# Expert slots in tiles of 64 and 32 tokens over a ring of five experts' weights, in a hybrid retention and attention trunk

## What is computed

```python
def hier_moe(h, w_group, w_router, w_gate, w_up, w_down):
    """Top-1 expert group, then top-2 experts inside it; gated-MLP experts."""
    ...
    weights = g_w * top_p / jnp.sum(top_p, axis=-1, keepdims=True)
    expert_idx = g_sel[:, None] * EXPERTS_PER_GROUP + top_i
    gates = jnp.sum(jax.nn.one_hot(expert_idx, N_EXPERTS, dtype=jnp.float32) * weights[..., None], axis=1)
    a = jnp.einsum('td,edf->tef', t, w_gate)
    u = jnp.einsum('td,edf->tef', t, w_up)
    hid = jax.nn.silu(a) * u * gates[:, :, None].astype(t.dtype)
    y = jnp.einsum('tef,efd->td', hid, w_down)
```

## Time and profile before

| | us |
|---|---|
| median of three runs | 1501.71 |
| lowest, highest | 1496.98, 1505.82 |
| the profiled execution | 1498.73 |
| its span, first to last instruction | 1496.6 |

### The profile page before, as it was taken

The page is one execution under the profiler, slowest core; times in us unless marked ns, Lnnn a source line. Parts: engine busy times, 40 slices in busy tenths (PEclk is TensorE's granted clock), DMA queues, the critical chain, the costliest instruction groups (busy, mean ns, idle before and its releaser), DMA issues.

```text
span 1496.6 us, 14033 instructions
## 1 busy us (share of the span) xinstructions
PE 1175.5 (79%) x5748; PEld 727.3 (49%) x5748; DVE 454.4 (30%) x736; ACT 242.8 (16%) x451; POOL 302.2 (20%) x232
## 2 busy tenths in 40 slices
PE   5999999999989982777779649688868296777790
PEld 4789698897967771322223224343434232322230
DVE  4212234322581033211112162635544311111114
ACT  4122221321421110000001010213213000000011
POOL 4133132231532202000222242100000200012124
PEclk9999999999999975988889959898988588998895
DMA  6141221321302353899995163100201769999825
GB/s 241 42 155 58 83 101 56 129 68 56 141 1 94 131 225 144 328 414 424 386 397 188 67 262 133 42 0 0 77 36 63 289 237 414 427 384 403 338 74 196
DMA packets 47176, 273.32 MB, mean 183 GB/s; under 512 B 8742, under 2 KB 8870, under 8 KB 33270
## 3 DMA queue, kind: packets, MB, share of 16 engines
q1 hardware_dynamic: 21168, 151.26, 25.7%
q0 software_dynamic: 13952, 77.15, 13.0%
q10 hardware_dynamic: 12000, 44.12, 7.4%
HBM read 277.28 MB, written 35.78 MB: 209 GB/s over the span
## 4 chain that ended last, share of the span: by engine, by line
PE 58%; issue 15%; DVE 11%; DMA 7%; POOL 6%; ACT 2%; ACTq 0%; POOLq 0%; SPq 0%; DVEq 0%
PE ps L665 19%; PE ps L828 14%; PE ps L849 6%; PE ps L886 4%; PE ps L972 4%; POOL ring_r L1672 4%; DMA ring<-in_w_gu,w_row 3%; PE ps L877 3%; DMA ring<-in_w_gu 2%; PE ps L814 2%; PE ps L798 2%; PE ps L751 2%; POOL slot_rows L1696 1%; DVE xT L1218 1%; DVE arena L1599 1%
## 5 line engine op out<-in xcount | busy, mean ns | idle before, releaser
L828 PE MATMUL ps<-ring,arena 128*64 128x512 f32 x768 | 258.4, 657 | 105.5 <-issue 99.5
L828 PEld LDWEIGHTS ps<-ring,arena 128*64 128x64 f32 x768 | 81.7, 151 | 272.9 <-issue 272.9
L665 PE MATMUL ps<-x_hi,ring_r 128*128 128x264 f32 x1024 | 190.9, 287 | 7.0 <-DVE xT_r L1206 7.0
L1672 POOL TENSOR_TENSOR ring_r<-ring,ring_r 128x1024 fp32r<-128x1024 f32 x56 | 134.2, 2408 | 301.5 <-ACT ring_r L999 301.5
L1218 DVE TENSOR_TENSOR arena<-ps,gains 128x512 f32<-128x512 f32 (+1 forms) x74 | 46.7, 673 | 397.8 <-PE ps L814 384.1
L665 PE MATMUL ps<-ring_r,x_hi 128*128 128x512 f32 (+1 forms) x480 | 155.8, 406 | 11.6 <-POOL ring_r L1672 11.6
L665 PEld LDWEIGHTS ps<-x_hi,ring_r 128*128 128x128 f32 x1024 | 160.3, 189 | 7.5 <-DVE xT_r L1206 7.3
L665 PE MATMUL ps<-xT_r,ring_r 128*128 128x264 f32 x512 | 146.1, 285 | 0.0
L828 PE MATMUL ps<-arena 128*64 128x512 f32 x256 | 133.9, 683 | 0.0
L849 PE MATMUL ps<-arena 128*64 128x512 f32 x512 | 116.9, 598 | 4.3 <-ACT arena L1121 4.3
L665 PEld LDWEIGHTS ps<-ring_r,x_hi 128*128 128x128 f32 (+1 forms) x480 | 84.3, 176 | 43.3 <-POOL ring_r L1672 13.1
(11 more groups left out here) (177 smaller groups left out, 1494.9 us busy)
## 6 DMA issues: line engine op xcount, KB each, us to landing
ring<-in_w_gu SPq DMA_DIRECT2D x24, 2048.0 KB, 14.1
arena<-in_w_down SPq DMA_DIRECT2D x32, 1024.0 KB, 10.4
ring<-in_w_ret SPq DMA_DIRECT2D x48, 512.0 KB, 3.6
arena<-in_w_gu SPq DMA_DIRECT2D x8, 2048.0 KB, 19.1
arena<-slot_rows ACTq DMA_DIRECT2D x32, 512.0 KB, 7.3
slot_out<-arena ACTq DMA_DIRECT2D x32, 512.0 KB
slot_rows<-arena ACTq DMA_DIRECT2D x8, 1024.0 KB, 4.0
ring<-in_w_ret_out SPq DMA_DIRECT2D x16, 512.0 KB, 4.5
```

Source lines behind the costliest of these rows:

```text
L665: last = mm(dst, a_parts[x], b_parts[y], start=(start and n == 0), stop=(stop and n == 2))
L828: last = mm(ps[half, b, :], xgT[:, k % 2, c, half], by_row(gu(2 * k + g))[:, c, :], start=(c == 0), stop=(c == KT - 1))
L1672: G.tensor_tensor(w_lo[slot][:, m], w_raw[slot][:, m], w_hi[to][:, m], ALU.subtract).then_inc(lo_made, 1)
```

## The change

The slot buffer is laid out anew. With c tokens an expert has ceil(c/32) tiles of 32. Pairs of tiles are "doubles" of 64 slots, an odd tile is a "single" of 32. There are 16 places for doubles and 16 for singles, and place j of the singles shares the weight buffer of place j of the doubles. If a double of an expert is in place j and the expert has a single, the single goes home to place j; singles without a home take free places. `PASSES` fixes twelve rounds, each with two halves of 64 slots: two doubles, or one double and two singles, or four singles in the last. A pass with singles therefore makes products with 32 stationary columns.

The weights have a ring of five buffers, all of which are prefetched with the weights of experts 0 to 4. GpSimd then "mends" these five with ten indirect DMAs, which write only partition 0 where the place really holds that expert. SP fills places 5 to 15, with the expert's number read from `e_of` into a register, when the single that used the buffer before has been computed. After both doubles of a pair of places have been computed, GpSimd "reloads" the two buffers for the singles; partition 0 alone is written where single and double are the same expert's.

Row loads and result stores become two DMAs of 64 rows. The slot rows and their transposes move into the buffer of `xT`. DVE's slot arithmetic grows from 13 to some 45 instructions.

The diff, cut to its core:

```diff
+TILE = 32
-SLOTS_W = 4
+W_SLOTS = 5
+AHEAD = 5
+PASSES = [(("d", 0), ("d", 1)), (("d", 2), ("s", 0)), (("d", 3), ("d", 4)), (("s", 2), ("d", 5)),
+          (("d", 6), ("s", 4)), (("d", 7), ("d", 8)), (("s", 6), ("d", 9)), (("d", 10), ("s", 8)),
+          (("d", 11), ("d", 12)), (("s", 10), ("d", 13)), (("d", 14), ("d", 15)), (("s", 12), ("s", 14))]
+ROUNDS = len(PASSES)
...
+        def double_arrived(eng, arrived, l, j):
+            eng.wait_ge(arrived[j % W_SLOTS], times_filled(l, j))
+            if j < AHEAD:
+                eng.wait_ge(mended[j // 2 > 0], 16 * (l + 1) * 2 * (AHEAD - 2 if j // 2 else 2))
+        def singles_arrived(eng, arrived, l, j):
+            n = j // 2
+            eng.wait_ge(arrived[n % 2], 32 * (l * (EXPERTS // 4) + n // 2 + 1))
...
+        def column_tiles(k):
+            for n, (kind, j) in enumerate(PASSES[k]):
+                if kind == "d":
+                    yield slice(BLK * n, BLK * n + BLK), j
+                else:
+                    for g in range(2):
+                        yield slice(BLK * n + TILE * g, BLK * n + TILE * g + TILE), j + g
...
+            def experts(l):
+                m = mo[l]
+                sp.wait_ge(m["eb_ready"], 1)
+                for j in range(AHEAD, EXPERTS):
...
+                    e = sp.value_load(e_of[0:1, l, j:j + 1], min_val=0, max_val=EXPERTS - 1)
+                    gu_d, dn_d = a["w_gu"][l], a["w_down"][l]
+                    if j >= W_SLOTS:
+                        round_full(sp, l, gu_bank(pass_of("s", j - W_SLOTS)), pass_of("s", j - W_SLOTS))
+                    gate_up_weights(l, j, gu_d[bass.ds(e, 1)].rearrange("a p c -> p (a c)"))
+                    if j >= W_SLOTS:
+                        round_full(sp, l, B_YB, pass_of("s", j - W_SLOTS))
+                    down_weights(l, j, dn_d[bass.ds(e, 1)].rearrange("a p c -> p (a c)"))
...
                     for c in range(KT):
-                        for g in range(2):
-                            half = slice(BLK * g, BLK * g + BLK)
-                            last = mm(ps[half, b, :], xgT[:, k % 2, c, half], by_row(gu(2 * k + g))[:, c, :],
+                        for cols, j in column_tiles(k):
+                            last = mm(ps[cols, b, :], xgT[:, k % 2, c, cols], by_row(gu(j))[:, c, :],
                                       start=(c == 0), stop=(c == KT - 1))
...
-                        act.dma_start(xg[:, k % 2, :], slot_rows.rearrange("(b p) c -> b p c", p=2 * BLK)[k])\
-                            .then_inc(m[f"x_in{k % 2}"], 16)
+                        for n, half in enumerate(PASSES[k]):
+                            act.dma_start(xg[BLK * n:BLK * n + BLK, k % 2, :],
+                                          slot_rows[half_rows(half):half_rows(half) + BLK, :]).then_inc(m[f"x_in{k % 2}"], 16)
...
+                for j in range(AHEAD):
+                    pool.wait_ge(gu_in[j % W_SLOTS], times_filled(l, j))
+                    others(a["w_gu"], gu(j), j).then_inc(mended[j // 2 > 0], 16)
+                    pool.wait_ge(down_in[j % W_SLOTS], times_filled(l, j))
+                    others(a["w_down"], flat(down[j % W_SLOTS]), j).then_inc(mended[j // 2 > 0], 16)
+                def reload(w, dst, arrived, k):
+                    for n in range(0, EXPERTS, 2):
+                        if pass_of("d", n + 1) == k:
+                            for j in (n, n + 1):
+                                others(w, dst(j), AHEAD + j).then_inc(arrived[n // 2 % 2], 16)
+                for k in range(ROUNDS):
+                    round_full(pool, l, gu_bank(k), k)
+                    reload(a["w_gu"], gu, gu_again, k)
+                    round_full(pool, l, B_YB, k)
+                    reload(a["w_down"], lambda j: flat(down[j % W_SLOTS]), down_again, k)
```

More of the change, by code:

```diff
@@ L290, in build @@
         cv = Carve()
[L291 to L294, removed]
+        gu_arena = cv(2, KT * 512)
+        down = [*(lambda d: [d[:, n] for n in range(AHEAD)])(cv(AHEAD, 2, D))]
         yo = cv(2, D)
@@ L846, in down_project @@
                         for c in range(2):
-                            for g in range(2):
-                                half = slice(BLK * g, BLK * g + BLK)
-                                last = mm(ps[half, b, :], hidT[:, c, half],
-                                          down[:, (2 * k + g) % SLOTS_W, c, 512 * n:512 * n + 512],
+                            for cols, j in column_tiles(k):
+                                last = mm(ps[cols, b, :], hidT[:, c, cols], down[j % W_SLOTS][:, c, 512 * n:512 * n + 512],
                                           start=(c == 0), stop=(c == 1))
@@ new lines, in experts @@
+                pos = v(POSN, nt, 16)
+                V_.tensor_tensor(pos, ps[:, 2, 0:16 * nt].rearrange("p (t e) -> p t e", e=16), before[:, 0:nt, :],
+                                 ALU.add).then_inc(free[2], 1)
+                step.done(V_.tensor_reduce(v(N_, 16), passed, X, ALU.add))
+                step.done(V_.memset(v(Z16, 16), 0.0))
+                step(V_.tensor_reduce(v(D_, 16), passed[:, :, 1:THRESH:2], X, ALU.add))
+                P0, P1 = v(PP, 17)[:, 0:16], v(PP, 17)[:, 1:17]
@@ new lines, in experts @@
+                step.done(V_.tensor_tensor(v(PC, nt, 16), pos, per_expert(v(CC, 16)), ALU.add))
+                step(V_.tensor_tensor(v(DBL, nt, 16), v(DBL, nt, 16), per_expert(v(CA, 16)), ALU.mult))
+                step(V_.tensor_tensor(v(PC, nt, 16), v(PC, nt, 16), v(DBL, nt, 16), ALU.add))
+                for at in (MA, MB):
+                    step.done(V_.tensor_tensor(v(at, nt, 16), v(at, nt, 16), v(PC, nt, 16), ALU.mult))
+                step.wait()
+                place = v(SLOT, 2, 5)
@@ new lines, in experts @@
+                for n, at in enumerate((MA, MB)):
+                    step.done(V_.tensor_reduce(place[:, n, 0:nt], v(at, nt, 16), X, ALU.add))
+                step.wait()
+                look = v(CMP, 16, THRESH).rearrange("p a b -> p (a b)")[:, 0:180].rearrange("p (a b) -> p a b", a=10)
+                if nt < 5:
+                    step(V_.memset(place[:, :, nt:5], 0.0))
+                step(V_.tensor_tensor(look, v(SLOT, 10).unsqueeze(2).to_broadcast([128, 10, 18]),
+                                      thr.unsqueeze(1).to_broadcast([128, 10, 18]), ALU.is_ge))
@@ new lines, in experts @@
+                step(V_.tensor_tensor(look, look, wt.unsqueeze(1).to_broadcast([128, 10, 18]), ALU.mult))
+                step(V_.tensor_reduce(v(LOOK, 10), look, X, ALU.add))
+                V_.scalar_tensor_tensor(slot_i[:, :, 0:nt], place[:, :, 0:nt], float(ENC_D), v(LOOK, 2, 5)[:, :, 0:nt],
+                                        ALU.add, ALU.add).then_inc(m["slot_ready"], 1)
+                eo, xo, dif, to, same = v(EO, 16), v(XO, 16), v(DIF, 16), v(TO, 21), v(SAME, 21)
+                step(V_.tensor_tensor(match, P1.unsqueeze(1).to_broadcast([128, 16, 16]), c16(num, 16), ALU.is_le))
```

247 lines of the change are left out of this document (144 added, 103 removed).

## The result

| | before | after |
|---|---|---|
| median | 1501.74 us (4 runs) | 1713.42 us (4 runs) |
| lowest, highest | 1496.98, 1505.82 | 1713.08, 1717.84 |
| ratio, with its 95% interval | | 1.142 [1.138, 1.146] |
| profiled execution, span | 1498.73, 1496.6 | 1717.84, 1715.9 |
| mean granted clock | 0.888 | 0.852 |

A forecast was written before the change was run, and what follows sets the result against it. Weight traffic was taken to bound about ten expert-loop rounds, TensorE the rest. Layer 0: 245.2 + 77 - 257.6 + 5.7 = +70.3; layer 1: +68.3; together +138.6 on 1498.7 gives 1637, median 1640 us, range 1475 to 1700.

The forecast's parts named there:

- What bounds, and the traffic: Expert loop: weight traffic bounds about ten rounds, TensorE the rest; weights fall from 51 expert loads to 32.
- The mixed passes: Six passes of one 64-column and two 32-column tiles: widths cannot overlap, 12.8 us per pass, 77 us per layer.
- The two rivals with overlap: In mixed passes, tiles overlap whatever their widths (1486 us, chance 0.36) or only partly (1543 us, chance 0.05).
- The routing chain: DVE's slot arithmetic before the scatters: 9.7 us instead of 4.0, delaying them by 5.7 us per layer.
- the mends hid as said: Before pass 0: four gating mends end 8.3 us after the scatters, hidden under 9.2 us of other work.
- The waits: TensorE's waits for reloads and SP's weights between products of the expert loop: 80.5 us per layer.
- restarts at half clock: TensorE restarting at 1.2 GHz after waits: nine at 1.8 us and the first at 2.6, 18.8 us a loop.
- The landing of a reload beside bulk loads: Passes 3, 6, 9: SP's simultaneous bulk loads add 6 us, between 0 and 7, to the reload wait: 10.5 us each.
- GpSimd's reaction: Expert loop: 0.1 us from the end of TensorE's product to GpSimd's first indirect reload DMA.
- the 4.5: Exposed wait for an empty gate/up reload in the expert loop: 0.1 + 1.3 + 3.1 = 4.5 us.
- SP's queue at passes 5, 8 and 10: Waits for weights that SP issues late in its single queue: 9.7 us each at 5 and 8, 2.3 at 10.
- Its slow end, 1686: Serial tiles in mixed passes with four width changes in a step and slow reload landings: 1686 us.

The follow-up runs named there:

- the two edits of before: Kernel before, each round's second block as two 32-column products beside the first's 64-column one: 1796.0 us; both blocks as two 32-column products each: 1507.6 us.

## Why the prediction was right and wrong

**What bounds, and the traffic: right.** Reloads and mends were nearly empty and the weight traffic fell. The profile's queue line shows it, and so does the DMA share of the loops.

**The mixed passes: right, in mechanism and size.** A step was forecast at 1.96 us and took 1.99. Gate/up 15.7 and down 7.8 were forecast, 15.9 and 7.95 measured where the clock was full. The two rivals with overlap (1486 and 1543 us) are excluded by the starts in the timeline and by the two edits of before, of which one costs some 290 us and one nothing. The rule of the Trainium skill that I weighed (TensorEngine Tiling (Array Packing), Key Properties: a change of tiling mode drains TensorE) agrees with these steps: 1.99 us for three tiles of two widths, 0.86 for two tiles of one. What the Trainium skill says in the section Packing small matmuls of TensorE: Matmul & The Clock Gate, that tiles overlap, holds here for tiles of one width: four of 32 overlap as well as two of 64 (3.61 and 3.58 us a down product). It does not hold for 64 beside 32 (7.95 us).

**The routing chain: close.** DVE's chain took 8.8 us where 9.7 were forecast, from these rows to be set beside the earlier trace rows:

```profile
567.59 0.44 DVE L1502 TENSOR_TENSOR arena<-arena,con 128x272 f32<-128x272 f32 x1
...
576.17 0.17 DVE L1570 SCALAR_TENSOR_TENSOR slot_i<-arena 128x10 int32<-128x10 f32 x1
```

That is 4.7 us more than before, not 5.7, and the mends hid as said. But the first expert product came 6.5 us (layer 0) and 7.3 us (layer 1) later. The row load is on this path. Its second half goes out 0.59 us later than the single load did, counted from the landing of the last scatter, and takes 4.03 us, where the single one took 3.27:

```profile
592.07 4.03 DMA xT<-slot_rows
```

I had costed that cut at nothing; it is 1.35 us in layer 0. From the last scatter's landing to the first product it is 1.6 and 2.2 us more than before, the rest of it a later start of the transposes that no row explains. With the shorter DVE chain set against it, 2.4 us are left over both layers.

**The waits: the step that failed.** By the sum the change was to cost 138.6 us; the two profiled executions differ by 219.1. The gap of 80.5 us (that the forecast waits of one layer sum to the same number is chance) is made up so: 36.1 and 38.1 in the two loops, 2.4 in the routing, 3.9 in the rest, which was not taken apart. In the loop of layer 0:

| wait ahead of | forecast, us | measured, us |
|---|---|---|
| gate/up 1 | 3.4 | 3.5 |
| gate/up 3, 6, 9 | 10.5 each | 15.1, 15.0, 15.1 |
| gate/up 4, 7, 11 | 7.1 each | 8.5, 8.5, 8.6 |
| gate/up 5, 8 | 9.7 each | 12.0, 12.1 |
| gate/up 10 | 2.3 | 4.9 |
| last down | 2.6 | 3.9 |
| sum | 80.5 | 107.2 |
| restarts at half clock | 18.8 | 24.7 |

The right waits stand in the right places, for the reasons given, but nearly all are longer. Three terms were mis-sized, and the first is the step that failed most.
- The landing of a reload beside bulk loads, the one place I had left to judgement. I added 6 us to 3.1 and called 0 to 7 the bounds. It landed 12.9 us after issue, together with the last of three bulk loads of 4.2 MB in all, and after 4.43 us when only these were light. The bounds were read from a row load that happened to land after 10.6 us; another row load in the same trace (L1116, issued at 700.5) took 13.2, beyond them. How the engines share their time between queues, and whether the reload's data or only its completion comes late, no run here separates. With a landing of 9.1 us in my sum this is 3 x 3.8 = 11.4 us a layer, the largest of the three.
- GpSimd's reaction. I took 0.1 us from TensorE's end to the first indirect load. The trace has 654.42 to 655.24, 0.8 us, once for each reload on the path: with seven of them (passes 3, 4, 6, 7, 9, 11 and the last down product) about 5 us a layer. The reloads without bulk loads beside them also landed after 3.5 to 3.9 us in layer 0, not 3.1, some 3 us a layer. That pass 1 came out right, at 3.5 us, is luck: both terms were short there too, and I had taken 1.1 us of cover off the 4.5, where the kernel without reloads shows 2.5 us between these two products.
- SP's queue at passes 5, 8 and 10. The load of pass 5 was to run beside nothing:

```profile
727.97 0.33 SPq L653 DMA_DIRECT2D arena<-in_w_down  x1
729.06 0.33 SPq L650 DMA_DIRECT2D arena<-in_w_gu  x1
729.58 0.33 SPq L653 DMA_DIRECT2D arena<-in_w_down  x1
731.01 0.33 SPq L650 DMA_DIRECT2D arena<-in_w_gu  x1
```

Between a down load and the gate/up load behind it lie 1.1 us, in which SP loads the expert's number into a register. I had costed the register loads at nothing, on the ground that SP waits longer for its semaphores; at these passes the semaphore had already come. And the next down and gate/up loads share the engines from 0.5 us later. 2.3 to 2.6 us a pass.

The restarts were 5.9 us short. I took 1.8 us for each, from products after the shorter waits of before; here mixed products after a wait take 17.6 to 18.7 us against 15.9, and that of pass 5 takes 10.01 against 6.87. The granted clock was 0.50 (1.2 GHz) from 669.47 to 674.00 and 1.00 (2.4 GHz) in the 4 us after. I also counted nine restarts for ten waits. That leaves 3.5 us of layer 0's 36.1. The mixed passes account for about as much: (15.9 - 6.87) + (7.95 - 3.58) is 13.4 us each, 0.6 more than the 12.8 of the sum, six times. Layer 1's loop, 2 us longer, was not taken apart.

The range was also cut too near. Its slow end, 1686, priced 4 us more of landing at 11 us; at three passes in each of two layers they are 24, so that end was 1698. The bound itself, 3.1 + 7 us, then lay below the landing measured.

## What to carry to other kernels

Give all tiles that TensorE is to run beside each other the same number of columns; if one tile of a product is narrow, cut the wide one to match. A transfer of nearly no bytes can cost the time of the bulk that is issued beside it, so before traffic is saved by adding small transfers, write down for each what the other queues issue within 2 us before and after it, and who waits for it. Starting 0.25 or 1.5 us ahead of the bulk it was late all the same; starting 7 us ahead it was not. When such a wait is moved, ask at once which small transfer the bulk will hit next: here it went from the gate/up reload in part to the row load, and then to the down reload.

## What the runs showed that I had not expected

- A change of width costs 0.13 us (7.95 to 7.43 us over four changes), but a lone wide tile among narrow pairs costs far more: 15.9 us for three tiles, 6.87 for two or four of one width.
- A small transfer on another queue does not get past bulk loads issued within 2 us of it, before it or after it: gate/up reloads with one real row landed after 12.8 to 13.0 us, down reloads after 13.6 to 15.9, halves of a row load after 14.0 to 14.5. Without bulk beside them the waited-for ones took 3.3 to 4.5 (reloads) and mostly about 4.0 (row load).
- GpSimd's first indirect load starts 0.8 us after the product that it waits for, and SP needs 1.1 us between two loads when it reads the next expert's number into a register between them, and 0.5 us when it does not.
